# Third piece of the next sublayer's weights, converted ahead into the idle slot behind an odd last chunk

## The reference

```
h, g = sublayer_input(x, norm_g[layer, 0], mod[:, 0])
x = x + MACARON_W * g * swiglu(h, ffn_w_gu[layer, 0], ffn_w_down[layer, 0])
...
y = stick_breaking_attention(h, ...)    # sb        y = rglru_block(h, ...)     # lru
y = _mla(h, ...); y = _conformer_conv(h, ...); y = _pool_mixer(h, ...); y = _sq_relu_mlp(h, ...)
```

## Time and profile before

| what | value |
|---|---|
| median of three runs | 2271.59 us (2268.57 to 2277.47) |
| profiled execution | 2272.67 us, its span 2270.8 us |
| TensorE busy, granted clock over the span | 2139.7 us, 94%; 0.982 of full |
| VectorE busy | 1612.3 us, 71% |
| ScalarE busy | 1223.9 us, 54% |
| DMA | 537.76 MB, mean 237 GB/s |

### The profile page before, as it was taken

The page is one execution under the profiler, slowest core; times in us unless marked ns, Lnnn a source line. Parts: engine busy times, 40 slices in busy tenths (PEclk is TensorE's granted clock), DMA queues, the critical chain, the costliest instruction groups (busy, mean ns, idle before and its releaser), DMA issues.

```text
span 2270.8 us, 36738 instructions
## 1 busy us (share of the span) xinstructions
PE 2139.7 (94%) x14508; PEld 1923.5 (85%) x14508; DVE 1612.3 (71%) x1786; ACT 1223.9 (54%) x1889; POOL 372.7 (16%) x551
## 2 busy tenths in 40 slices
PE   3999998999999996999998999999998999999998
PEld 3998877998899795998777998969987998878987
DVE  7787755777678677777765886647976887765544
ACT  3544555544554465654565654546644664575643
POOL 2121000121021003121000320422312230000210
PEclk9999999999999998999999999999999999999999
DMA  9998773798789763799642897745996698332652
GB/s 345 333 315 318 242 257 115 279 325 315 217 303 338 204 229 63 260 315 344 209 142 62 304 324 273 190 112 201 329 325 194 226 330 311 111 128 86 199 196 103
DMA packets 298485, 537.76 MB, mean 237 GB/s; under 512 B 11487, under 2 KB 188434, under 8 KB 298352
## 3 DMA queue, kind: packets, MB, share of 16 engines
q1 hardware_dynamic: 262048, 356.55, 48.9%
q0 software_dynamic: 36032, 178.33, 22.0%
q10 hardware_dynamic: 272, 1.05, 0.1%
HBM read 530.12 MB, written 1.11 MB: 234 GB/s over the span
## 4 chain that ended last, share of the span: by engine, by line
PE 83%; DVE 7%; ACT 5%; issue 2%; DMA 1%; SPq 0%; DVEq 0%; ACTq 0%
PE bk L1390 12%; PE bk L1391 12%; PE bk L1392 12%; PE bk L1286 10%; PE bk L1288 10%; PE bk L1287 10%; PE bk L1274 1%; PE bk L1276 1%; PE bk L1275 1%; DVE w_lo L1809 1%; PE bk L1650 1%; DMA first_mod<-in_mod_w 1%; ACT w_hi L822 1%; PE bk L1367 1%; PE bk L1369 1%
## 5 line engine op out<-in xcount | busy, mean ns | idle before, releaser
L1809 DVE TENSOR_TENSOR w_lo<-raw,w_hi 128x1024 fp32r<-128x1024 f32 (+5 forms) x720 | 841.8, 1195 | 461.7 <-ACT w_hi L822 459.6
L822 ACT ACTIVATE w_hi<-raw 128x1024 fp32r<-128x1024 f32 (+5 forms) x720 | 686.0, 977 | 663.4 <-PE bk L1288 346.5
L1390 PE MATMUL bk<-a_hi,w_hi 128*128 128x256 f32 x2362 | 672.5, 285 | 7.4 <-DVE a_lo L1919 5.2
L1391 PE MATMUL bk<-a_lo,w_hi 128*128 128x256 f32 x2362 | 670.9, 284 | 0.0
L1392 PE MATMUL bk<-a_hi,w_lo 128*128 128x256 f32 x2362 | 670.7, 284 | 0.0
L1390 PEld LDWEIGHTS bk<-a_hi,w_hi 128*128 128x128 f32 x2362 | 454.7, 193 | 9.8 <-DVE a_lo L1919 5.6
L1391 PEld LDWEIGHTS bk<-a_lo,w_hi 128*128 128x128 f32 x2362 | 454.9, 193 | 0.0
L1392 PEld LDWEIGHTS bk<-a_hi,w_lo 128*128 128x128 f32 x2362 | 454.9, 193 | 0.0
L1830 DVE SCALAR_TENSOR_TENSOR mod_acc<-mod_raw,cact,mod_acc 128x1536 f32<-128x1536 f32 x182 | 338.6, 1860 | 6.2 <-DMA mod_raw<-in_ada_w 5.2
L1286 PE MATMUL bk<-w_hi,hid_hi 128*128 128x512 f32 x816 | 324.1, 397 | 0.0
L1287 PE MATMUL bk<-w_lo,hid_hi 128*128 128x512 f32 x816 | 322.7, 395 | 0.0
(11 more groups left out here) (364 smaller groups left out, 2925.1 us busy)
## 6 DMA issues: line engine op xcount, KB each, us to landing
raw<-in_ffn_w SPq DMA_DIRECT2D x128, 1024.0 KB, 6.8
mod_raw<-in_ada_w POOLq DMA_DIRECT2D x128, 768.0 KB, 7.0
raw<-in_ffn_w_gu SPq DMA_DIRECT2D x88, 1024.0 KB, 7.3
mod_raw<-in_mod_w POOLq DMA_DIRECT2D x80, 768.0 KB, 7.2
raw<-in_ffn_w_down SPq DMA_DIRECT2D x40, 1024.0 KB, 7.7
first_mod<-in_mod_w SPq DMA_DIRECT2D x16, 768.0 KB, 12.0
raw<-in_sb_w_qkv SPq DMA_DIRECT2D x12, 1024.0 KB, 7.7
raw<-in_conv_w_pw SPq DMA_DIRECT2D x12, 1024.0 KB, 6.0
```

Of the source, the lines that this page charges most:

```text
L822: ins = act.activation(o(w_hi[:, p % OPS, :]), r(raw[:, c % RAWS, :]), ACT.Copy)
L1390: pe.matmul(o, wh, a_hi[:, f, :], start=(f == 0), stop=False)
L1391: pe.matmul(o, wh, a_lo[:, f, :], start=False, stop=False)
L1809: ins = dve.tensor_tensor(o(w_lo[:, p % OPS, :]), r(raw[:, c % RAWS, :]), o(w_hi[:, p % OPS, :].bitcast(F32)), ALU.subtract)
```

## The change

The third piece of the five sublayers that begin behind an odd last chunk goes into the idle slot. So it can be made before the first and second, and `early` is true for all sublayers but the first. As the third piece now lies in slot 3, the fourth goes to slot 2, and slots 2 and 3 stay exchanged until the next odd last chunk (`flips`, `slot`). `at_place` gives the order of making: third, first, second. `made` and `slot_free` correct the counts that are waited for, and `freed` makes SyncE wait for one piece more where the order within a chunk no longer is that of the counts: for the first and every fourth chunk of sb and ffn1, and for the fifth chunk of each of the five.

```
         def early(n):
-            return n > 0 and kinds[n - 1] not in ("ffn1", "lru")
+            return n > 0
...
+        flips = [sum(kd in ("ffn1", "lru") for kd in kinds[:n]) % 2 for n in range(len(kinds))]
+        turned_over = {2 * z["c"] + 2 for z in stages[1:] if flips[z["n"]] != flips[z["n"] - 1]}
+        def slot(p):
+            n = [z["n"] for z in stages if 2 * z["c"] <= p][-1]
+            return p % OPS ^ (flips[n] if p % OPS >= 2 else 0)
+        first_of = {p - 2 for p in turned_over}
+        def at_place(s):
+            return s + 2 if s in first_of else s - 1 if s - 1 in first_of or s - 2 in first_of else s
+        def made(p):
+            return p + 2 if p in first_of or p - 1 in first_of else p - 1 if p - 2 in first_of else p + 1
+        def slot_free(p):
+            return p - 2 if p in turned_over else p + 1
...
+            def freed(c):
+                first = [2 * z["c"] for z in stages if z["c"] <= c and (z["c"] == c and z["kind"] in ("ffn1", "sb") or z["c"] == c - RAWS)]
+                return 2 * c + 2 + any(p in first_of for p in first)
             def chunk(c, src, view, i=0):
-                sp.wait_ge(lo_ready, 2 * c + 2 + 8 * i)
+                sp.wait_ge(lo_ready, freed(c) + 8 * i)
...
-                for p in range(a, b):
+                for p in map(at_place, range(a, b)):
-                    act.wait_ge(piece_used, p + 1 + 8 * i)
+                    act.wait_ge(piece_used, slot_free(p) + 8 * i)
...
                     x_half(0, w + 11)
-                    pieces(p + 61, p + 70)
+                    pieces(p + 61, p + 71)
                     x_half(1, w + 11)
...
-                pe.wait_ge(lo_ready, 2 * RAWS + p + 1 + 8 * i)
+                pe.wait_ge(lo_ready, 2 * RAWS + made(p) + 8 * i)
-                    wh, wl = (z[:, p % OPS, 512 * r:512 * r + 512] for z in (w_hi, w_lo))
+                    wh, wl = (z[:, slot(p), 512 * r:512 * r + 512] for z in (w_hi, w_lo))
...
                             if st["end"]:
                                 mod_finish(st["end"], w + 12)
+                            pieces(p + 70, p + 71)
                             second_half(g, w + 12, c + 34)
```

More of the change, by code:

```diff
@@ L574, in _ @@
                             kt = 4 * (b % 2)
-                            sp.wait_ge(lo_ready, 2 * (c + b) + 2)
+                            sp.wait_ge(lo_ready, freed(c + b))
                             for s in range(2):
@@ L821, in pieces @@
                     for o, r in split(p):
-                        ins = act.activation(o(w_hi[:, p % OPS, :]), r(raw[:, c % RAWS, :]), ACT.Copy)
+                        ins = act.activation(o(w_hi[:, slot(p), :]), r(raw[:, c % RAWS, :]), ACT.Copy)
                     ins.then_inc(hi_ready, 2 if p in double else 1)
@@ L1240, in _ @@
                     x_half(0, w + 5)
-                    pieces(p + 29, p + 34)
+                    pieces(p + 29, p + 35)
                     x_half(1, w + 5)
@@ L1309, in last_pieces @@
                         for r in range(2):
-                            wh, wl = (y[:, (p + z) % OPS, 512 * r:512 * r + 512] for y in (w_hi, w_lo))
+                            wh, wl = (y[:, slot(p + z), 512 * r:512 * r + 512] for y in (w_hi, w_lo))
                             xh, xl = (y(kt + 2 * z + r)[:, s] for y in xs)
@@ L1359, in first_gate_up @@
                         if f == 0:
-                            first_feature([(job_banks(w)[:, m, :], *(z[:, (p + m // 2 * 2) % OPS, P * (m % 2):P * (m % 2) + P]
+                            first_feature([(job_banks(w)[:, m, :], *(z[:, slot(p + m // 2 * 2), P * (m % 2):P * (m % 2) + P]
                                                                      for z in (w_hi, w_lo))) for m in range(4)], act_from)
@@ L1365, in first_gate_up @@
                             o, s = job_banks(w)[:, m, :], 256 * r + P * (m % 2)
-                            wh, wl = (z[:, (p + m // 2 * 2) % OPS, s:s + P] for z in (w_hi, w_lo))
+                            wh, wl = (z[:, slot(p + m // 2 * 2), s:s + P] for z in (w_hi, w_lo))
                             pe.matmul(o, wh, a_hi[:, f, :], start=(f == 0), stop=False)
@@ L1381, in gate_up @@
                         if act_from is not None and q == 0 and f == 0:
-                            first_feature([(job_banks(w)[:, m, :], *(z[:, p % OPS, P * m:P * m + P] for z in (w_hi, w_lo)))
+                            first_feature([(job_banks(w)[:, m, :], *(z[:, slot(p), P * m:P * m + P] for z in (w_hi, w_lo)))
                                            for m in range(2)], act_from)
@@ L1388, in gate_up @@
                             o = job_banks(w)[:, q // 2 * 2 + m, :]
-                            wh, wl = (z[:, p % OPS, 256 * r + P * m:256 * r + P * m + P] for z in (w_hi, w_lo))
+                            wh, wl = (z[:, slot(p), 256 * r + P * m:256 * r + P * m + P] for z in (w_hi, w_lo))
                             pe.matmul(o, wh, a_hi[:, f, :], start=(f == 0), stop=False)
@@ L1502, in go @@
                         def go(p, r, f, xs, first, last):
-                            wh, wl = (z[:, p % OPS, :] for z in (w_hi, w_lo))
+                            wh, wl = (z[:, slot(p), :] for z in (w_hi, w_lo))
                             xh, xl = (z(f) for z in xs)
@@ L1525, in _ @@
                             p = 2 * (c + 2 * n) + q
-                            pe.wait_ge(lo_ready, 2 * RAWS + p + 1)
+                            pe.wait_ge(lo_ready, 2 * RAWS + made(p))
                             for r in range(2):
                                 if n == 0 and q + r == 0:
-                                    first_feature([(job_banks(w)[:, m, :], w_hi[:, p % OPS, a:a + P], w_lo[:, p % OPS, a:a + P])
+                                    first_feature([(job_banks(w)[:, m, :], w_hi[:, slot(p), a:a + P], w_lo[:, slot(p), a:a + P])
                                                    for m, a in enumerate(starts)], nq)
@@ L1545, in _ @@
                             pe.wait_ge(lo_ready, 2 * RAWS + p + r + 1)
-                            wh, wl = (z[:, (p + r) % OPS, :] for z in (w_hi, w_lo))
+                            wh, wl = (z[:, slot(p + r), :] for z in (w_hi, w_lo))
                             xh, xl = (z(3 + r) for z in C)
@@ L1559, in _ @@
                             for r in range(2):
-                                wh, wl = (z[:, (p + r) % OPS, 512:] for z in (w_hi, w_lo))
+                                wh, wl = (z[:, slot(p + r), 512:] for z in (w_hi, w_lo))
                                 xh, xl = (z(3 + r)[:, P * a:P * a + P] for z in C)
@@ L1687, in pool_products @@
                             for r in range(2):
-                                wh, wl = (z[:, (2 * c + r) % OPS, 256 * q:256 * q + 256] for z in (w_hi, w_lo))
+                                wh, wl = (z[:, slot(2 * c + r), 256 * q:256 * q + 256] for z in (w_hi, w_lo))
                                 xh, xl = a_hi[:, 2 * q + r, s], a_lo[:, 2 * q + r, s]
@@ L1801, in pieces @@
             def pieces(a, b, i=0):
-                for p in range(a, b):
+                for s in range(a, b):
+                    p = at_place(s)
                     c = p // 2
@@ L1806, in pieces @@
                         continue
-                    dve.wait_ge(hi_ready, p + 1 + 8 * i)
+                    dve.wait_ge(hi_ready, s + 1 + 8 * i)
                     for o, r in split(p):
-                        ins = dve.tensor_tensor(o(w_lo[:, p % OPS, :]), r(raw[:, c % RAWS, :]),
-                                                o(w_hi[:, p % OPS, :].bitcast(F32)), ALU.subtract)
+                        ins = dve.tensor_tensor(o(w_lo[:, slot(p), :]), r(raw[:, c % RAWS, :]),
+                                                o(w_hi[:, slot(p), :].bitcast(F32)), ALU.subtract)
                     ins.then_inc(lo_ready, 2 if p in double else 1)
```

## The result

| | before | changed |
|---|---|---|
| median | 2274.77 us | 2281.01 us |
| lowest to highest, 8 runs each | 2268.57 to 2278.85 | 2276.13 to 2287.84 |
| profiled execution, its span | 2272.7, 2270.8 | 2276.1, 2274.3 |

The change made the kernel slower: 1.0028 times the time before, 95% interval 1.0015 to 1.0040, some 6.4 us, where 4.2 us less were forecast. Run again later it gave 1.0030 (1.0019 to 1.0042). The forecast time, 2267.4 us, lies 13.6 us under the measured one. Of these, 3.2 are the kernel before, whose median was 2271.59 over three runs and is 2274.77 over eight; the other 10.4 are the change.

A forecast was written before the change was run, and what follows sets the result against it. TensorE was taken as the bound (busy 94% of the span), so only its stops or lower clock pay. 8.1 + 1.1 - 2.2 - 2.8 = 4.2 us gained, from 2271.6 to 2267.4 us; range 2261 to 2276, 8 in 10.

The forecast's parts named there:

- Removed from the starts: Starts of sublayers 1, 3, 4, 5 and 6: TensorE's stops for a_lo go, 8.1 us gained.
- The half-clock rest: First gate-up of sublayer 3: 1.1 us of lower-clock loss expected to stay, leaving a gain of 2.3 us.
- Moved ahead of the tail: Ends before sublayers 3, 4 and 6: `mod_finish` ahead of the last subtraction, 0.37 us each, 1.1 us gained.
- A new wait in sublayers 3 and 5: Jobs behind the first gate-up: four banks per feature make conversions come in a burst, TensorE waits for w_lo, 2.2 us lost.
- the fold: VectorE's mod_t (1.77 us) in sublayer 3, expected to delay w_lo during the burst: 0.8 us lost; 0 in sublayer 5.
- The queue behind the third piece: Ends of sublayers 2 and 4: third piece's late transfer holds the first two pieces and the tail, 2.8 us lost.
- the full price: Loss if the second chunk lands as late as in the trace in both sublayers 3 and 5: 5.6 us.
- the third rival: Sublayer changes bound by the third piece's transfer: price 14.6 us against 7.0, 7.6 us slower, 2279 us; chance 0.10.

The follow-up runs named there:

- the exact count: Changed kernel with TensorE's wait for w_lo in the looped gate-up jobs counted as in the kernel before; ratio 1.0021 to the kernel before.
- the two exact waits together: Changed kernel with TensorE's w_lo wait counted exactly and the first chunk of sublayers 3 and 5 issued one piece earlier; ratio 1.0000 to the kernel before.

## Why the prediction was wrong

The terms were the right ones; two sizes were wrong, one of them by a factor of four.

- **Removed from the starts**, forecast 8.1 us: measured 0.8 (interval of sublayer 1, whose stop is gone), 3.4 and 3.5 (first gate-up 12.34 and 12.77 us to the second job's first matmul, against 15.75 and 16.22 counted alike), 0.5 in sublayer 4 (0.86 less the new 0.34, where I said 0.4) and 0.5 in 6. That is 8.7. The 0.5 in sublayer 4 is luck of this execution: with the 1.81 us of the same kernel run again that start loses 0.9. The half-clock rest that I left in sublayer 3 wasn't there, since the stretch fell ahead of the job, and in sublayer 5, where I wrote "without the stop I expect full clock", 0.93 was granted, for the clock fell in the new wait.
- **Moved ahead of the tail**, forecast 1.1: 0.3 is seen at the end of sublayer 3 (TensorE's wait for the normed x is 1.44 us, before 1.77) and 0.1 at the end of 5. At the end of 2 it was lost behind the late piece, as the text had it for that case.
- **A new wait in sublayers 3 and 5**, forecast 2.2: the second and third job lose 1.85 us in each (first job's end to the fourth job's start 24.88 us, before 23.04), 3.7. I gave the first wait the 0.46 us of sublayer 2; it was 1.59. I followed the bank order and SyncE's counts and didn't read `made(p)` in the looped jobs: 1.13 us per sublayer, shown by the exact count. For the fold I took 0.8; no wait of over 0.25 us shows behind the third job.
- **The queue behind the third piece**, forecast 2.8: this is the step that failed. The tail's product came 3.9 us late at the end of sublayer 2 (584.92; 581.0 would be 581.91 less the 0.9 us that the sublayer began earlier) and 7.6 at the end of 4 (916.22 against 908.6: that sublayer began 1.4 us later and had won 0.5 at its start), 11.5 together. I had set the full price at 5.6 from the landings of the trace, halved it since "Three rows speak for 0 and two, in just the ffn1 sublayers, for the full price", and left out what I had named myself, that the later first chunk can add 2.8 us at each. With both in full it would have been 11.2.

So 8.7 + 0.4 - 3.7 - 11.5 = -6.1 us, where the medians differ by 6.2 and the ratio says 6.4. That they meet so closely is partly luck: the lower clock behind the late product at the end of 4 (6.6 us from it to the first matmul, before 5.7) is not in the sum, and the fifth piece's wait in sublayer 4 alone moves it by 1.5. The profiled execution shows only 3.5 of it, since its sublayer 6 is 4.0 us shorter with 0.5 of stop removed: the clock was full where it was halved before. These are windows of the kernel before and, behind them, of the changed kernel some 7 us later, near the same work:

```profile
1184.00:1188.00 4.00, 4.00 (x16) 2.68 (x14) 1.47 (x7) 2.42 (x9) 0.00 (x0) 0.57 0.33 33
1204.40:1211.20 6.80, 5.36 (x30) 3.24 (x28) 1.61 (x6) 2.51 (x5) 0.00 (x0) 0.51 0.00 0
```

```profile
1190.50:1194.50 4.00, 3.47 (x23) 2.34 (x22) 2.91 (x12) 2.88 (x12) 0.00 (x0) 1.00 0.24 28
1210.90:1217.70 6.80, 4.19 (x34) 3.06 (x35) 1.61 (x4) 2.41 (x6) 0.00 (x0) 1.00 0.00 0
```

The mistake behind the size is one of kind. I took the landing times as draws of chance ("single stretches of slow transfer, not a queue that is always full") and so gave the third rival, the third piece's transfer as the bound, 0.10. It came true, at 11.5 us instead of its 14.6. Each of the two slow landings stood behind the same GpSimd DMA, issued 1 us ahead of the second chunk in one place and 2.4 in the other, and the landings of 7.7 and 7.2 us had none in the same stretch. That stood in the trace of the kernel before and spoke for a price paid in every execution instead of two in five, and the runs bear it out: where the third piece came first and the gate row stayed, ScalarE's wait came back each time (9.32, 9.20 and 10.20 us at the end of 2; 7.22 and 6.96 with the first chunk early), and with the gate row moved or in runs at most 1.93 us were left. Not every slow landing has this cause: from 1452 to 1481 us six chunks of the kernel before took 12.0 to 16.7 us with no gate row beside them, but with GpSimd's copies of `stack`, 71 KB each, under way. No run here tells why.

The Trainium skill (DMA: Bandwidth & Descriptors, Why small descriptors are slow) charges each DMA operation 32 bytes of descriptor metadata, beside some 3 cycles for each packet. An estimate from the metadata, with 64 values on each of 16 engines and so 2 KB at a sixteenth of its 436 GB/s, is 0.1 us for the whole DMA. In the trace of the changed kernel the packets of that DMA begin over 1.0 us. Both figures are of the DMA itself; what it does to others is larger, some 7.5 us of lateness for the weights beside it (16.2 against 8.7).

What stays open: whether the slow stretch is made by the reads of single values or by their writes to HBM (the run length changed both), and why the two exact waits together are not faster than one. On the first the trace of the changed kernel has a hint: the gate row's 4 KB are 16 packets of 256 bytes that all begin between 567.5 and 568.5 us, and the low rate comes behind them (48 GB/s from 569 to 575). That speaks for what follows the reads, but no run tells the two apart.

## What to carry to other kernels

Before a step is moved to need a transfer earlier, look at each slow landing of the trace and ask what else was issued beside it: here a landing behind one of the program's own DMAs was slow in every trace (13.6 to 17.1 us in eleven), so its whole price belonged in the sum. A piece made ahead in an in-order queue should stand behind the pieces that are needed sooner; with that DMA in place the idle slot gave its gain with the third piece last (0.9961) and lost it with the third piece first (1.0028). Where an order of production changes, read every wait that counts pieces, in the loops above all: an offset that is right for one turn of a loop asked for one piece too many in another. On TensorE it was right in the first turn and too much in the later ones (1.13 us in each of two sublayers); on SyncE it was needed in the later turns and held up the first chunk (issued at 562.68 us instead of 559.33).

## What the runs showed of the hardware

- Behind one DMA of 1024 single 4-byte values, 4 KB in all, 48 GB/s arrived over 6 us; in 128 runs of 8 values, at the same place, the rate was 348 GB/s.
- The slow stretch travels with that DMA: 56 GB/s at 611 to 617 us when it was issued at 608.17; 188 against 365 GB/s at 786 to 796 us with and without it in sublayer 4.
- The granted clock fell within TensorE's wait of 9.08 us (0.53 from 914 to 925 us), and the 16 transposes behind it took 3.67 us, where those at the start of 3 took 2.51 at full clock. So such a wait costs some more in the work behind it.
